# A two-block transformer kernel: eight buffers in modulation, banks and norms in attention's inputs, and the last feature tile in token halves

## The reference, cut to what matters

```
mod_lat, mod_ctx = silu(c) @ w_mod + b_mod, silu(c_ctx) @ w_mod + b_mod
hx = rms_norm(x)   * (1 + sc1)  + sh1          # 512 tokens
hc = rms_norm(ctx) * (1 + csc1) + csh1         # 256 tokens
ak, av, qkv, db, da, aq, z, gate = split(h @ w_in)
q = rope(rms_norm(aq, q_norm_w)); k = rope(rms_norm(ak, k_norm_w))   # 8 heads, 2 key heads; no rope on ctx
attn = softmax(q k^T / sqrt(128)) v            # keys of all 768 tokens
... gated delta rule, merge, conv FFN, then two mixer/MLP layers ...
h = h + square(relu(z @ w_mlp1)) @ w_mlp2      # the last product of all
out = h * rsqrt(mean(h * h, -1) + eps) * final_norm_g
```

## Time and profile before

| | us |
|---|---|
| median of three runs (2614.57 to 2618.03) | 2617.45 |
| profiled execution | 2617.6 |
| its span | 2615.7 |
| TensorE busy | 2534.7 (97%) |
| VectorE, ScalarE, GpSimd busy | 1384.2, 1019.4, 274.9 |
| mean granted clock | 0.987 |

### The profile page before, as it was taken

The page is one execution under the profiler, slowest core; times in us unless marked ns, Lnnn a source line. Parts: engine busy times, 40 slices in busy tenths (PEclk is TensorE's granted clock), DMA queues, the critical chain, the costliest instruction groups (busy, mean ns, idle before and its releaser), DMA issues.

```text
span 2615.7 us, 46226 instructions
## 1 busy us (share of the span) xinstructions
PE 2534.7 (97%) x19810; PEld 2062.0 (79%) x19810; DVE 1384.2 (53%) x1952; ACT 1019.4 (39%) x1695; POOL 274.9 (11%) x228
## 2 busy tenths in 40 slices
PE   6999999999999899999999999999999999999998
PEld 4766787778888788788888887788888876888887
DVE  4445698545677433466653556553453455552542
ACT  3245766433333322343333337532223347321232
POOL 0210102223331000101111010100000010000001
PEclk9999999989999999999999999999999999999999
DMA  7100310141003222322332221232332221232222
GB/s 269 58 18 21 117 57 33 47 160 59 4 4 130 87 97 97 129 81 97 97 98 95 90 81 57 78 98 98 97 98 97 89 65 56 90 97 97 97 97 72
DMA packets 64714, 222.90 MB, mean 85 GB/s; under 512 B 7168, under 2 KB 7552, under 8 KB 64384
## 3 DMA queue, kind: packets, MB, share of 16 engines
q1 hardware_dynamic: 63936, 218.39, 25.1%
q10 hardware_dynamic: 576, 1.57, 0.2%
HBM read 213.64 MB, written 6.29 MB: 84 GB/s over the span
## 4 chain that ended last, share of the span: by engine, by line
PE 88%; DVE 6%; ACT 3%; issue 2%; DMA 1%; POOL 0%; SPq 0%; POOLq 0%; DVEq 0%; ACTq 0%
PE ps L321 59%; PE ps L2668 6%; PE ps L1625 5%; PE ps L331 3%; PE ps L741 2%; PE ps L715 1%; PE ps L1650 1%; PE ps L1667 1%; PE ps L1631 1%; DMA ring<-in_w_mod_first 1%; DVE o_tok L1517 1%; DVE w_lo L299 1%; PE ps L2722 1%; PE ps L731 1%; PE ps L2753 1%
## 5 line engine op out<-in xcount | busy, mean ns | idle before, releaser
L299 DVE TENSOR_TENSOR w_lo<-ring,w_hi 128x1024 fp32r<-128x1024 f32 (+1 forms) x339 | 417.7, 1233 | 825.6 <-ACT w_hi L291 825.6
L291 ACT CAST w_hi<-ring 128x1024 fp32r<-128x1024 f32 (+1 forms) x339 | 353.9, 1044 | 931.5 <-PE ps L321 827.8
L321 PE MATMUL ps<-u_hi,w_hi 128*128 128x512 f32 x864 | 337.9, 391 | 2.5 <-DVE u_lo L2478 2.5
L321 PE MATMUL ps<-u_lo,w_hi 128*128 128x512 f32 x864 | 336.8, 390 | 0.0
L321 PE MATMUL ps<-u_hi,w_lo 128*128 128x512 f32 x864 | 336.8, 390 | 0.0
L321 PE MATMUL ps<-mid_hi,w_hi 128*128 128x512 f32 x688 | 267.6, 389 | 0.0
L321 PE MATMUL ps<-mid_lo,w_hi 128*128 128x512 f32 x688 | 267.6, 389 | 0.0
L321 PE MATMUL ps<-mid_hi,w_lo 128*128 128x512 f32 x688 | 267.6, 389 | 0.0
L321 PEld LDWEIGHTS ps<-u_hi,w_hi 128*128 128x128 f32 x864 | 162.5, 188 | 37.7 <-issue 3.2
L321 PEld LDWEIGHTS ps<-u_hi,w_lo 128*128 128x128 f32 x864 | 162.6, 188 | 34.1
L321 PEld LDWEIGHTS ps<-u_lo,w_hi 128*128 128x128 f32 x864 | 162.6, 188 | 34.0 <-issue 0.5
(11 more groups left out here) (468 smaller groups left out, 4599.9 us busy)
## 6 DMA issues: line engine op xcount, KB each, us to landing
ring<-in_w_up SPq DMA_DIRECT2D x44, 512.0 KB, 3.5
ring<-in_w_in SPq DMA_DIRECT2D x42, 512.0 KB, 3.4
ring<-in_w_merge SPq DMA_DIRECT2D x32, 512.0 KB, 3.5
ring<-in_w_mlp1a SPq DMA_DIRECT2D x32, 512.0 KB, 3.4
ring<-in_w_mlp2a SPq DMA_DIRECT2D x32, 512.0 KB, 3.5
ring<-in_w_mlp1b SPq DMA_DIRECT2D x32, 512.0 KB, 3.4
ring<-in_w_mlp2b SPq DMA_DIRECT2D x32, 512.0 KB, 3.5
ring<-in_w_gdn_in SPq DMA_DIRECT2D x24, 512.0 KB, 3.5
```

The source lines that it names most:

```text
L291: nc.scalar.copy(w_hi[:, slot, 0:width], ring[:, n % RING, 0:width]).then_inc(*hi_ok.one())
L299: nc.vector.tensor_tensor(w_lo[:, slot, 0:width], ring[:, n % RING, 0:width], as_f32(w_hi[:, slot, 0:width]), ALU.subtract).then_inc(*lo_o ...
L321: mm = nc.tensor.matmul(dst[:, a:b], w[wi][:, k * P:(k + 1) * P], src[xi][:, k0 + k, a:b], start=start and k == wi == xi == 0, stop=stop a ...
```

## The change

In modulation four more buffers (`more`) stand beside the ring, so that eight units of `w_mod` may be on their way. The sixteen units leave the common numbering of units; the first attention unit is number 0, issued before the fifteenth unit of `w_mod`. Shift and scale of two tiles share one bank, with two stationary tiles (`cs` and `cs_scale`, whose values stand in columns 2 and 3), so there are four row copies and four turns instead of eight. The token sums stand after the second unit and the rows after the fourth. VectorE multiplies `x` by the rows in one pass of 768; scale and shift are applied in ScalarE (five tiles) or VectorE (tiles 3, 5 and 7), the high part is a plain copy and the low part a plain subtraction.

In attention's inputs item 1 goes to pair 0, item 2 to pair 1, and so on; the copy of the value tokens stands ahead of a split; the reciprocal and the multiply of the key heads are made for 512 and 256 tokens apart, and the rotation waits for the first part. In attention the last head's value product of tiles 0 and 1 stands ahead of the last transposes. The last product and the last norm become one stage: the last feature tile is made in two halves of 256 tokens, each with its own addition, squares, sums, root, rows, multiplies and stores.

```diff
+BUFFERS = 8
-                    for n in range(MOD_FIRST + RING):
-                        m = n - RING
-                        if m >= 0 and whole_unit(m):
-                            sp.wait_ge(*unit_used.at(m + 1))
-                        ...
+                    for j in range(MOD_FIRST):
+                        if j == FIRST_AFTER:                       # 14
+                            sp.wait_ge(*mod_used.at(BUFFERS + 1))
+                            sp.dma_start(ring[:, 0, 0:units[0].shape[1]], units[0]).then_inc(loaded[0], 16)
+                        if j >= BUFFERS:
+                            sp.wait_ge(*mod_used.at(j - BUFFERS + 1))
+                        ...                                        # ring for slots 0-3, more for 4-7
+                    for n in range(1, RING):
+                        sp.wait_ge(*mod_used.at(BUFFERS + n + 1))
+                        ...                                        # units 1 to 3, rest of the tables after 2
 # ScalarE
+                    def whole_part(k):
+                        ...                                        # waits: x_normed, mod, h_low of k - 4
+                        for p, (a, b) in enumerate(parts):
+                            mm = nc.scalar.activation(whole[:, k % 4, a:b], x[:, k, a:b], ACT.Identity,
+                                                      scale=mod[:, KD + k, p:p + 1], bias=mod[:, k, p:p + 1])
+                    def high_part(k):
+                        nc.scalar.copy(h[0][:, k, :], whole[:, k % 4, :]).then_inc(*h_hi.one())
-                        if k in (5, 7):
-                            row_copy((k - 5) // 2)
+                    row_copy(0); whole_part(0); row_copy(1); high_part(0); whole_part(1); row_copy(2)
+                    high_part(1); whole_part(2); high_part(2); split_hi(act, 0); high_part(3); whole_part(4)
+                    row_copy(3); high_part(4); high_part(5); whole_part(6); high_part(6); high_part(7)
 # TensorE
+                    for j in range(MOD_FIRST):
+                        group(j)                                   # one unit, four products
+                        if j == 1:
+                            ...                                    # token sums, were after group 3 (unit 7)
+                        if j == 3:
+                            ...                                    # rows
+                        if j in columns_after:                     # (4, 9, 12)
+                            mod_columns(columns_after.index(j))
+                    w = unit(pe)
+                    feature(0)
+                    mod_columns(n_pairs - 1)
+                    for k in range(1, KD):
+                        mm = feature(k)
 # VectorE
+                    normed(0); bias(0); normed(1); normed(2); normed(3); bias(1); low_part(0); whole_part(3)
+                    normed(4); bias(2); low_part(1); normed(5); low_part(2); split_lo(dve, 0); low_part(3)
+                    whole_part(5); bias(3); normed(6); low_part(4); normed(7); whole_part(7)
+                    low_part(5); low_part(6); low_part(7)
 # attention's inputs
+            def banks_of(n):
+                return pair(0 if n == 0 else (n + 1) % 2)
-                                pe.wait_ge(*evac.at(max(n, 2)))
+                                pe.wait_ge(*evac.at(n))
+                                if i == 0:
+                                    pe.wait_ge(*evac.at(2))
-                                    pe.wait_ge(*n_ok.at(i + 1))
+                                    pe.wait_ge(*n_ok.at(2 * i + 1))
+                                nc.scalar.copy(vtok, ps[:, 2:2 + TT, 0:KV_HEADS * P]).then_inc(*evac.one())
                                 split_hi(act, 3)
-                                nc.scalar.copy(vtok, ps[:, 2:2 + TT, 0:KV_HEADS * P]).then_inc(*evac.one())
+                                for p, (a, b) in enumerate(key_parts):     # (0, 512), (512, 768)
+                                    ...                                    # reciprocal, then multiply
 # attention
-                                pe.wait_ge(*sig("gemm_evac").at(i - 1))
+                                pe.wait_ge(*sig("gemm_evac").at(-i))
+                            elif i == n_items - 1:
+                                pe.wait_ge(*o_ok.at(h))
+                                values(h, 0, t - 1)
                             pe.wait_ge(*p_ok.at(i + 1))
 # last product and norm: stage_last, TensorE
+                        for u in range(per):                       # 2 units, 8 k each, 256 tokens
+                            ws.append(unit(pe))
+                            for k in range(8):
+                                mm = part_of_unit(ws[u], u, 0, k)
+                        mm.then_inc(*first_done.one())
+                        for u in range(per):
+                            for k in range(8):
+                                mm = part_of_unit(ws[u], u, 1, k)
+                                if 8 * u + k == SUMS_AFTER:        # 4
+                                    first_sums()
+                                    token_sums(0)
+                                elif 8 * u + k == ROWS_AFTER:      # 7
+                                    pe.wait_ge(*done.at(LAST))
+                                    rows(0)
+                            mm.then_inc(*unit_used.one())
+                        token_sums(1)
+                        rows(1)
 # VectorE and GpSimd, for each half p
+            on_pool = ((2, 4, 6), (2, 5))                          # the others on VectorE
```

More of the change, by code:

```diff
@@ L256, in build @@
                 add(f"{name}_{layer}")
-        n_split = [n - sum(whole[:n]) for n in range(len(units))]
         loaded = [top.enter_context(nc.semaphore(f"unit_loaded{s}")) for s in range(RING)]
@@ L335, in product_tok @@
             return mm
-        def mod_rows(pe, half, dst):
-            w = unit(pe)
-            for k in range(4):
-                mm = nc.tensor.matmul(dst[32 * k:32 * k + 32, :], cs[:, 4 * half + k, :],
-                                      w[:, k * 2 * P:(k + 1) * 2 * P], start=half == 0, stop=half == 1)
-            mm.then_inc(*unit_used.one())
         norm_in = [sig(f"norm_in{k}") for k in range(KD)]
@@ L479, in _, with normed @@
                 def _(dve):
+                    def normed(k):
+                        nc.vector.tensor_tensor(x[:, k, :], x[:, k, :], rstd, ALU.mult).then_inc(*xn_ok.one())
                     def bias(p):
-                        for i, m in ((2 * p, 2 * p), (2 * p + 1, KD + 2 * p)):
-                            dve.wait_ge(*turned.at(i + 1))
+                        dve.wait_ge(*turned.at(p + 1))
+                        columns = bank(p)[:, 2 * P:2 * P + 8].rearrange("p (c v) -> p c v", v=4)
+                        for part in range(2):
+                            m = part * KD + 2 * p
```

492 lines of the change are left out of this document (298 added, 194 removed).

## The result

The kernel before took 2616.01 us (median of 6 runs, 2606.35 to 2628.93), the changed kernel 2593.35 us (6 runs, 2591.79 to 2606.23). The time lies 8.9 us under the forecast of 2602.2 and 4.2 us under the range's low end. Of the 8.9 us, 7.5 are the gain (22.7 us between these medians, forecast 15.2), and 1.4 come from the kernel before, whose six runs have a lower median than the three that the forecast started from. Later runs gave a smaller gain. Over all comparisons of several runs the changed kernel has 25 runs with a median of 2598.62 us, the kernel before 100 runs with 2616.14 us: 17.5 us apart (a resampling of the runs gives 14.8 to 20.8).

A forecast was written before the change was run, and what follows sets the result against it. TensorE, holding the last-ending chain for 88% of the span, was taken as the bound. Gains 6.9 + 4.2 + 0.3 + 1.0 + 2.8 = 15.2 off 2617.6 gave 2602.4, against the median 2602.2; range 2597.5 to 2609.5.

The forecast's parts named there:

- Modulation (M): Modulation up to the start of the value product: product ends at 50.3 us, gain 6.9, bounds 3.2 to 9.2.
- Value copy and clock behind it: Attention's inputs: 2.6 us wait for the value copy goes, clock stays up behind it; gain 4.2, bounds 2.6 to 4.3.
- Split norms, to attention's start: Attention's inputs: key head's norm in two parts ends a 1.4 us TensorE wait; gain 0.3, bounds -0.3 to 1.4.
- Attention's end: Before the last transposes: value tiles fill TensorE's 0.98 us wait; gain 1.0, bounds 0.5 and 1.1.
- Last feature tile: Kernel's end: first half's multiplies and stores lie under the second half's products; gain 2.8, bounds 1.5 and 4.0.
- The middle: From the first product behind attention to the last weight cast: untouched, nothing costed, 0 us.
- Step D: Modulation's features: clock falls, four features at 1.93 us, the rest at 1.05; product ends at 50.3, bounds 48.0 and 54.0.
- Step A: Modulation: sums behind unit 1, rows behind unit 3; rows end at 24.0 us, 8.2 us earlier than 32.24.
- Step C: Modulation's transfers: eight buffers bring units at 1.25 us each, DMA hidden; features start at 37.6 us against 46.3.
- Rival 1: Modulation: clock stays up from its first rise, product ends at 48.0, gain 9.2 there; 2600.0 us in all; chance 0.18.
- rivals 2 and 4: Clock low to modulation product's end (2606.0 us, chance 0.13); low through the value matmuls too (2625.9 us, chance 0.03).
- Rival 3: Modulation: eight outstanding transfers share the engines, x and unit 0 late; gains nothing or loses 1; 2610.2 us; chance 0.08.

The follow-up runs named there:

- norm_order: Changed kernel with VectorE's list in attention's inputs in another order, split norms kept, nothing left out; 2595.02 us (0.9904).
- whole_norms: Changed kernel with each key head's reciprocal and multiply in one piece of 768 again; one run, 2603.15 us.
- both: Changed kernel with norm_order's VectorE list plus seven unread matmuls in modulation where TensorE waited; 2593.38 us (0.9894).
- t_before: The kernel before, unchanged, run again as a candidate against itself; 2615.29 us (1.0004).
- late_rows: Changed kernel with token sums and rows both behind unit 7, first columns behind unit 8; one run, 2601.37 us.
- rest_only: Kernel before with the new attention inputs, attention and last stage, but the old modulation; 2606.38 us (0.9968).

## Why the prediction was right or wrong

The gain of each step by the marks, once for the first pair of profiles and once as a mean: the profiles of the two kernels and the two halves that lack the part, less those that have it (us, rounded one by one).

| Step | forecast | first pair | mean | how the mean comes about |
|---|---|---|---|---|
| Modulation (M) | 6.9 | 9.8 | 10.7 | 57.61 (5 profiles) less 46.96 (6) |
| Value copy and clock behind it | 4.2 | 4.3 | 4.0 | 12.5 less 8.5 |
| Split norms, to attention's start | +0.3 | -1.3 | -1.6 | 18.4 less 19.7, and 0.4 of clock behind item 4 |
| Attention's end | 1.0 | 1.1 | 1.8 | 113.0 less 111.3 |
| Last feature tile | 2.8 | 3.0 | 3.1 | 25.0 less 21.9 |
| Sum of the steps | 15.2 | 16.9 | 17.9 | |
| The middle | 0 | 7.9 | 2.9 | 2324.7 (kernel before, 3) less 2321.9 (changed, 4) |

Two terms of the sum failed. Modulation's 6.9 us, bounds 3.2 to 9.2, was 10.7. And the middle, which was put at nothing without a reason, gave 7.9 us in the pair of profiles that goes with the first medians; that is more than modulation's error of 2.9 in the same pair, and without it the first gain of 22.7 us would have stayed within the range. The sum of the steps, 17.9, agrees with the 17.5 us between the pooled medians. The mechanisms held: rows early, VectorE as the next bound, a fall of the clock near 33 us and its return under features, no wait for the value copy. Sizes and one sign were off.

Three slips of the working are small beside this. Step D's own terms give 50.5 and not 50.3 (46.3 and four features at 1.05). It is set against the chain's 57.20, where the timeline has the value product start at 57.03. And item 4's first matmul before the change started at 105.35, not at the 105.9 that adds a start and a duration of the chain; against 105.35 the same working gives a loss of 0.2 us for the split norms and not a gain of 0.3.

**Modulation, steps A and D.** Step A put the end of the rows at 24.0, and they ended at 22.1: the sums began at 15.16 instead of 16.1, since unit 0 had landed at 12.98 (13.85 in the first profile of the kernel before), units 2 and 3 took 1.9 us instead of 2.2, and the rows 2.46 instead of 2.94, as the clock rose at 21.5. All that hangs on the rows came earlier: the features began at 35.26 instead of 37.6, the last low part was ready at 44.64 instead of 46.9. Step D had the mechanism, with four features at the low level; there were three (42.01 is the start of feature 3), another 0.9 us, and with it M is 47.2 instead of 50.3. The bound 48.0 was no bound, because it took the last low part at 46.9 for fixed.

Over the eight profiles with this modulation and nothing added (norm_order and whole_norms included) the rows end at 22.1 to 23.5, the last low part at 44.4 to 46.0, and M is 46.0 to 47.7. So the early unit 0 was luck of the first profile (13.1 to 14.0 in the other seven, 13.6 to 13.9 with the old modulation), while M is no luck: the rows are early in all, the clock came back before the last low part in all, and where it came back soonest M follows the last low part by 1.5 us, where the old modulation took 4.8 to 5.3. Step C's "the DMA is then hidden" was wrong as well: units 12 and 14 were waited for 2.07 and 1.81 us with the engines busy 1.02 to 1.04. Those two waits are what the clock fell behind. Rival 1, the clock stays up, did not happen in the changed kernel; both shows what it would have given, 44.95. Nor did rivals 2 and 4: the clock was back by 42.2 in all eight. Rival 3, that eight outstanding transfers share the engines, is refuted: unit 0 landed at 13.6 us on average in these eight and at 13.7 with the old modulation, and with four outstanding M is 5.7 us later.

On the clock the Trainium skill ("TensorE: Matmul & The Clock Gate", Part 1) speaks of a fall after an idle stretch; here it fell behind 1.93 us of work in 4 with no idle time longer than 2.07 us, and with seven matmuls in those holes it stayed up. So the trace differs from the rule if idle is read as a long stretch of doing nothing.

**Split norms, wrong sign.** I had added 0.1 us for each of four more instructions. The cost was elsewhere: the sine product stood behind both parts of head 1, and the second product of head 0 took 1.21 us beside GpSimd's pass against 0.48 alone. I had the right queue ("VectorE's queue is full"), and I named the sine product as next late, but took it at 1 us of wait. It was 1.75 us, with 0.70 before it for rotation 1. norm_order shows that the order is the cause: the same instructions in another order give 2.5 us, with the 1.21 us still in them. The Trainium skill ("SBUF — State Buffer", "SBUF: two separate sides") has VectorE and GpSimd hold the shared ports for a whole instruction each. The 1.21 us agree with that nearly: the product starts at 82.67, GpSimd's pass ends at 83.60, and 0.28 us are left to 83.88, where the product takes 0.48 alone. That is 0.2 us short of a wait for the whole pass, and no run here tells why.

**Attention's inputs and end, last tile** came within their bounds, but for attention's end: the 1.8 holds a fall of the clock that two of five profiles of the old form had (114.0 and 114.1 us against 112.4) and none of the new form. Without it the gain is 1.1.

**The range.** "The middle 2300 us are untouched; nothing in them is costed" was the real error of the range. Untouched code differed by up to 12.7 us between profiles, nearly all of it in one stretch of 500 us, and the time at the low clock level in it went along. In the first pair the changed kernel had 10.2 us less of that; at 0.39 us each this is 4.0 of the 7.9 us, and the other 3.9 stay open. Single runs of the changed kernel have a standard deviation of 4.9 us. The first six had clocks of 0.985 to 0.992, four of them 0.990 or more. At a reported clock of 0.987 the changed kernel's five runs average 2601.2 and the kernel before's 22 runs 2614.6 us, at 0.990 seven and five runs average 2594.3 and 2612.0: 13 and 18 us apart. (The reported clock leaves out the low level ahead of the first rise, see below, so this comparison is rough.) A median of six as low as 2593.35 is rare even among the pooled 25 runs (about one in a hundred draws), so I can't call it plain luck as shown; what made its clock higher stays open. Three later comparisons gave 15.4, 22.5 and 17.7 us between medians.

## What to carry to other kernels

When a chain behind one engine is moved forward, every bound in the sum that was computed from the old start moves too; a range whose end is "features follow the last low part" must let that low part move. Before an instruction is split on a full in-order queue, write down which of the pieces somebody waits for, and place those pieces; split without a new order, it lost 1 us, and in the new order it won 1.5 over the undivided norms. And give untouched stages the spread that repeated runs show: two more profiles of the kernel before would have shown 4 us of it.

## What the runs showed of the hardware

The granted clock is not a function of the program. t_after is the changed kernel again. From 88 to 92 us TensorE was busy 1.55 us in the first profile of the changed kernel and 1.56 in t_after; the clock stayed up behind it in the first and was 0.58 from 92 to 96 in the other, which is these two rows (the first profile, then t_after):

```profile
92.00:96.00 4.00, 4.00 (x16) 3.00 (x17) 2.27 (x3) 0.00 (x0) 3.92 (x3) 1.00 0.38 130
```
```profile
92.00:96.00 4.00, 4.00 (x10) 2.51 (x9) 1.98 (x3) 0.00 (x0) 3.92 (x3) 0.58 0.38 131
```

A clock of 1.00 in a row of stretches is not always a level that was granted. In t_before the first change of clock on record is the rise at 52.4 us, and the stretches ahead of it read 1.00; but two units take 2.22 us and a feature's first pair 1.01 there, against 0.64 a unit and 0.62 a pair at full (both). So it was at the low level ahead of the rise, though TensorE was busy for 2.58 to 4.00 us of every four from 14 us on. The rise came 5 us behind the start of the features at 47.38. First the stretch, then the timeline:

```profile
42.00:46.00 4.00, 2.58 (x19) 0.92 (x19) 3.96 (x8) 2.42 (x5) 0.00 (x0) 1.00 1.04 420
```
```profile
43.36 2.22 PE L343 MATMUL ps<-ring,silu_c_buf 128*32 128x256 f32 x16 [1.84 <-DMA ring<-in_w_mod_first]
...
47.38 1.01 PE L321 MATMUL ps<-h_hi,w_hi 128*128 128x512 f32 x2
```

The kernel before first rose at 34.0, 52.1 and 52.4 us in its three profiles, the changed one at 21.5 to 23.7 in its four. The other profiles go the same way: all eleven with sums and rows ahead of unit 4 rose at 21.5 to 24.5; of the six with them behind unit 7, five rose at 34.0 or later (late_rows, with eight buffers, at 41.7), and rest_only rose at 18.2 and was low again from 21.6 to 52.3. So the first rise goes with the place of sums and rows. I had not costed such a shift, and why it is so stays open.

A reciprocal of fp32 on VectorE took 3.35 us for 512 elements a partition, 1.75 for 256 and 4.95 for 768, so splitting it costs 0.15 us.

The fastest version beside others on one chip is both, at 2593.38 us against 2598.60 for the changed kernel. From norm_order's 2595.02 its time is not told apart; its M is.
